# Two experts' weight tiles through one ring of seven buffers: the first nine loads of each pair in another order

## The reference

```python
for e in range(N_EXPERTS):
    out = out + gates[:, e:e + 1] * swiglu(tok, w_gate_up[e], w_down[e])
# swiglu(h, wgu, wd): gate, up = split(h @ wgu); (silu(gate) * up) @ wd
# wgu: 1024 x 7168, wd: 3584 x 1024, float32: 44 MB for each expert
```

## Time and profile before

| | |
|---|---|
| median of 3 executions | 1496.53 us (1495.41 to 1497.82) |
| the profiled execution, its own time | 1497.91 us |
| its span from the first to the last instruction | 1496.1 us |
| TensorE busy | 1346.0 us, 90% of the span |
| VectorE / ScalarE busy | 673.5 / 520.2 us |
| moved by DMA | 474.28 MB, mean 317 GB/s |

### The profile page before, as it was taken

How to read it: one execution, slowest core, us unless ns; L and a number is a source line. 1 busy time by engine, 2 the same in 40 slices (tenths; PEclk the granted TensorE clock), 3 DMA queues, 4 the chain that set the end, 5 groups by cost and what they waited for, 6 DMA issues and landing times.

```text
span 1496.1 us, 25369 instructions
## 1 busy us (share of the span) xinstructions
PE 1346.0 (90%) x11187; PEld 966.0 (65%) x11188; DVE 673.5 (45%) x754; ACT 520.2 (35%) x566; POOL 35.8 (2%) x66
## 2 busy tenths in 40 slices
PE   3899899999999897999999999999888889887776
PEld 2674578888789646777776777766675665443332
DVE  5953344445354526655453755443764553100002
ACT  2323433343253604444442454443553442000001
POOL 3000000000010002000000000000000000000000
PEclk8989999999999997999999999999998999999999
DMA  8874794554495214689999989999999999999994
GB/s 285 323 289 156 285 394 170 203 189 169 169 340 205 75 57 171 224 337 410 412 411 412 384 319 411 411 410 412 399 351 411 414 411 411 412 412 413 412 413 190
DMA packets 206791, 474.28 MB, mean 317 GB/s; under 512 B 9986, under 2 KB 10030, under 8 KB 206670
## 3 DMA queue, kind: packets, MB, share of 16 engines
q1 hardware_dynamic: 199968, 470.83, 81.2%
q10 hardware_dynamic: 6702, 1.71, 0.5%
HBM read 471.47 MB, written 1.05 MB: 316 GB/s over the span
## 4 chain that ended last, share of the span: by engine, by line
PE 64%; DMA 16%; SPq 12%; DVE 3%; ACT 2%; issue 1%; ACTq 1%; POOL 0%; POOLq 0%; DVEq 0%
PE ps L2355 39%; DMA ring<-in_moe_w_down_dram 13%; SPq L511 12%; PE ps L2667 6%; PE ps L2679 5%; DMA ring<-in_ada_w_dram 3%; PE ps L2528 2%; PE ps L2331 2%; PE ps L2166 1%; PE ps L2230 1%; PE ps L2291 1%; PE ps L2622 0%; PE ps L2659 0%; PE ps L2252 0%; PE ps L2456 0%
## 5 line engine op out<-in xcount | busy, mean ns | idle before, releaser
L1918 DVE TENSOR_TENSOR ring_lo<-ring,w 128x2048 fp32r<-128x2048 f32 x126 | 288.2, 2290 | 186.3 <-ACT w L1063 149.0
L1063 ACT ACTIVATE w<-ring 128x2048 fp32r<-128x2048 f32 x126 | 240.4, 1912 | 221.0 <-PE ps L2355 208.8
L2667 PE MATMUL ps<-ring,arena 128*32 128x128 f32 (+1 forms) x5376 | 240.2, 294 | 28.6 <-DMA ring<-in_moe_w_gate_up_dram 24.8
L2667 PEld LDWEIGHTS ps<-ring,arena 128*32 128x32 f32 (+1 forms) x5376 | 183.3, 115 | 89.2 <-DMA ring<-in_moe_w_gate_up_dram 34.8
L2355 PE MATMUL ps<-ring_lo,x_hi 128*128 128x512 f32 x592 | 231.2, 391 | 0.0
L2355 PE MATMUL ps<-w,x_hi 128*128 128x512 f32 x336 | 135.3, 403 | 4.5 <-DVE ring_lo L1918 2.6
L1541 DVE TENSOR_TENSOR ring_lo<-ring,w_hi 128x2048 fp32r<-128x2048 f32 x42 | 95.6, 2290 | 89.0 <-ACT w_hi L788 89.0
L2355 PE MATMUL ps<-w,x_lo 128*128 128x512 f32 x336 | 131.3, 391 | 0.0
L2355 PEld LDWEIGHTS ps<-ring_lo,x_hi 128*128 128x128 f32 x592 | 111.3, 188 | 21.2
L2679 PE MATMUL ps<-ring,tri 128*32 128x512 f32 (+1 forms) x448 | 72.6, 662 | 38.1 <-DMA ring<-in_moe_w_down_dram 36.1
L788 ACT ACTIVATE w_hi<-ring 128x2048 fp32r<-128x2048 f32 x42 | 78.8, 1908 | 49.1 <-PE ps L2355 42.1
(11 more groups left out here) (399 smaller groups left out, 1694.3 us busy)
## 6 DMA issues: line engine op xcount, KB each, us to landing
ring<-in_moe_w_gate_up_dram SPq DMA_DIRECT2D x112, 2048.0 KB, 17.5
ring<-in_moe_w_down_dram SPq DMA_DIRECT2D x56, 2048.0 KB, 18.3
ring<-in_ada_w_dram SPq DMA_DIRECT2D x24, 2048.0 KB, 11.1
ring<-in_ffn_w_gate_up_dram SPq DMA_DIRECT2D x14, 2048.0 KB, 11.6
ring<-in_ffn_w_down_dram SPq DMA_DIRECT2D x7, 2048.0 KB, 7.7
ring<-in_sb_w_qkv_dram SPq DMA_DIRECT2D x6, 2048.0 KB, 8.6
ring<-in_s_w_out_dram SPq DMA_DIRECT2D x2, 2048.0 KB, 7.7
ring<-in_sb_w_out_dram SPq DMA_DIRECT2D x2, 2048.0 KB, 14.5
```

Of the source, the lines that this page charges most:

```text
L1063: act.activation(half3(h).bitcast(F32R), ff_half(gran(pair_place(*main_granule(n))), half), ACT.Copy).then_inc(whi_done, 1)
L1918: dve.tensor_tensor(ff_half(ring_lo[place % RING][:, :], half).bitcast(F32R), ff_half(gran(place), half), half3(h), ALU.subtract).then_inc ...
L2667: ins = pe.matmul(dst[width * r:width * r + width, 0:cols], x[:, k, 0:width], weights[:, k, cols * r:cols * r + cols], start=k == 0, stop= ...
```

## The change

Positions 2 to 7 of each pair's list change places. Written out:

| position | 0 | 1 | 2 | 3 | 4 | 5 | 6 | 7 | 8 | 9 | 10 | 11 | 12 | 13 | 14 |
|---|---|---|---|---|---|---|---|---|---|---|---|---|---|---|---|
| buffer | 2 | 3 | 4 | 5 | 6 | 0 | 1 | 2 | 3 | 4 | 5 | 6 | 0 | 1 | 2 |
| before | ag0 | au0 | ag1 | au1 | ad0 | bg0 | ad1 | bu0 | ag2 | au2 | bg1 | ad2 | bu1 | ag3 | bd0 |
| after | ag0 | au0 | ad0 | ag1 | au1 | bg0 | bu0 | ad1 | ag2 | au2 | bg1 | ad2 | bu1 | ag3 | bd0 |

From position 8 on the lists are the same. The code that runs when the routing does not allow pairs took its places from position in the old list too; `expert_place` keeps the first five granules of that code in the buffers where the loads ahead now put them. That code isn't executed for these inputs.

```
 def pair_order():
 
-    order = [("ag", 0), ("au", 0), ("ag", 1), ("au", 1), ("ad", 0), ("bg", 0), ("ad", 1), ("bu", 0), ("ag", 2)]
+    order = [("ag", 0), ("au", 0), ("ad", 0), ("ag", 1), ("au", 1), ("bg", 0), ("bu", 0), ("ad", 1), ("ag", 2)]
     for f in range(2, FB):
         order += [("au", f), ("bg", f - 1), ("ad", f), ("bu", f - 1)]
         if f < FB - 1:
...
+def expert_place(g):
+
+    return N_MOE + {2: 3, 3: 4, 4: 2}.get(g, g)
...
-                swiglu_weights(moe_w_gate_up[0][0], moe_w_down[0][0], lambda g: N_MOE + g,
+                swiglu_weights(moe_w_gate_up[0][0], moe_w_down[0][0], lambda g: expert_place(g),
                                lambda g: (N_MOE + g) // RING, AHEAD)
...
-                                wait_used(act, N_MOE + gate_at(f), moe_turn(gate_at(f)))
+                                wait_used(act, expert_place(gate_at(f)), moe_turn(gate_at(f)))
```

More of the change, by code:

```diff
@@ L592, in _ @@
                     swiglu_weights(gate_up[bass.ds(expert * D, D), :], downs[bass.ds(expert * FF, FF), :],
-                                   lambda g: N_MOE + g, lambda g: e * (PER_EXPERT // RING) + (N_MOE + g) // RING)
+                                   lambda g: expert_place(g), lambda g: e * (PER_EXPERT // RING) + (N_MOE + g) // RING)
             for tt in range(TT):
@@ L1210, in w_round @@
                                 return
-                            wait_landed(act, N_MOE + g, moe_turn(g))
+                            wait_landed(act, expert_place(g), moe_turn(g))
                             if h >= 3:
@@ L1214, in w_round @@
                                 if part:
-                                    wait_used(act, N_MOE + before, moe_turn(before))
+                                    wait_used(act, expert_place(before), moe_turn(before))
                                 else:
                                     act.wait_ge(h0_read, split * PER_EXPERT + before + 1)
-                            act.activation(half3(h).bitcast(F32R), ff_half(gran(N_MOE + g), half), ACT.Copy
+                            act.activation(half3(h).bitcast(F32R), ff_half(gran(expert_place(g)), half), ACT.Copy
                                            ).then_inc(whi_done, 2 if g in plain else 1)
                         def silu_main(f):
-                            wait_used(act, N_MOE + gate_at(f), moe_turn(gate_at(f)))
+                            wait_used(act, expert_place(gate_at(f)), moe_turn(gate_at(f)))
                             if f:
@@ L2037, in product_item @@
                                 dve.wait_ge(m_silu, e * FB + f + 1)
-                                wait_used(dve, N_MOE + up_at(f), moe_turn(up_at(f)))
+                                wait_used(dve, expert_place(up_at(f)), moe_turn(up_at(f)))
                                 if f:
@@ L2065, in w_rest @@
                                 dve.wait_ge(*tail_read[g])
-                            dve.tensor_tensor(ff_half(ring_lo[(N_MOE + g) % RING][:, :], half).bitcast(F32R),
-                                              ff_half(gran(N_MOE + g), half), half3(h), ALU.subtract
+                            dve.tensor_tensor(ff_half(ring_lo[expert_place(g) % RING][:, :], half).bitcast(F32R),
+                                              ff_half(gran(expert_place(g)), half), half3(h), ALU.subtract
                                               ).then_inc(wlo_done, 2 if g in plain else 1)
@@ L2950, in gate_product @@
                         def gate_product(f, ch, width):
-                            n = N_MOE + gate_at(f)
+                            n = expert_place(gate_at(f))
                             wait_landed(pe, n, moe_turn(gate_at(f)))
@@ L2956, in up_product @@
                         def up_product(f, ch, width):
-                            n = N_MOE + up_at(f)
+                            n = expert_place(up_at(f))
                             wait_landed(pe, n, moe_turn(up_at(f)))
@@ L2982, in down_product @@
                         def down_product(f, ch, width):
-                            n = N_MOE + down_at(f)
+                            n = expert_place(down_at(f))
                             wait_landed(pe, n, moe_turn(down_at(f)))
@@ L3019, in tail_in @@
                         def tail_in(g, f, at, done):
-                            n = N_MOE + g
+                            n = expert_place(g)
                             wait_landed(pe, n, moe_turn(g))
@@ L3051, in halves @@
                         def halves(g, half, cols):
-                            low = ff_half(ring_lo[(N_MOE + g) % RING][:, :], half)
+                            low = ff_half(ring_lo[expert_place(g) % RING][:, :], half)
                             return [w.rearrange("p (k n) -> p k n", n=cols) for w in (half3(2 * g + half), low)]
                         def main_in(g, f, bank, free):
-                            n = N_MOE + g
+                            n = expert_place(g)
                             if f:
```

## The result

The changed kernel takes 1486.41 us (median of 4 executions, 1482.16 to 1487.72) against 1497.17 us for the kernel before (1495.41 to 1498.13): 10.8 us less, a ratio of 0.9925 with a 95% interval of 0.9902 to 0.9947. Measured a second time (6 executions beside 11 of the kernel before) the ratio was 0.9928 (0.9913 to 0.9942). Forecast were 9.5 us and 1487.0 us.

What follows compares the result with a forecast made beforehand. The routed SwiGLU was taken as bound by its 352 MB of weight loads, the winnable time being queue gaps. Terms of 2.5 + 2.7 + 4.3 = 9.5 us off 1496.5 gave 1487.0 us, range 1483.6 to 1492.2.

Steps and rivals of the forecast that it cites:

- The reading of the holes: Queue gaps at the start of pairs 0 to 2, of 20.2, 10.8 and 6.7 us: loads wait for buffers.
- The split into TensorE's half and the queue's: In a wide pair with a tail, PE sets the pace of the first half and DMA of the second.
- the lead: How much earlier loads land: 5.1 to 6.5 us in pair 0, cut to 1.7 to 3.2 after bu 2.
- Pair 0: Pair 0's share of the gain: 2.5 us (1.7 to 3.2), left after bu 2 and passed on to pair 1.
- Pair 1: Pair 1's share of the gain: 2.7 us (1.9 to 3.4), left after bu 2; PE's 4.4 us of waits cover it.
- Pair 2: Pair 2's share of the gain: 4.3 us, with ad 2 landing 3.7 to 4.5 us earlier.
- TensorE at pair 2's start: PE's down 0 product in pair 2: DVE's gate-up product precedes its splits, 0.2 us to gain, counted as nothing.
- The price of a starved load: A load issued into an empty queue lands 7.5 to 9.0 us later, mean 8.2.
- A: Rival: starved loads bg 2 and bu 2 cost 10.7 us or more, only pair 2 gains 4.3: 1492.2; chance 0.07.
- C: Rival: in pair 2 too the hole only moves, to bg 2 and bu 2; no measurable change, 1496 us; chance 0.07.
- B: Rival: starved loads at the lower price and PE's waits in pairs 0 to 2 used up: 12.9 us, 1483.6; chance 0.05.
- D: Rival: ad 1 late for ACT's split in each wide pair, 15.3 us lost if hit fully, 1502; chance 0.05.

Runs made afterwards that it cites:

- swap_only: Kernel before with only bu 0 and down 1 changing places in each pair's list: ratio 1.0008 to the kernel before.
- release_f2: Changed kernel with block 2 of the list also in order of release (bg1 au2 bu1 ad2), in all pairs: ratio 0.9927 to the kernel before.
- release_f23: Changed kernel with blocks 2 and 3 also in order of release: ratio 0.9900 to the kernel before, repeated 0.9893.
- pair2_only: Changed kernel with the new order in pair 2 alone, the old one in the other pairs: ratio 0.9969 to the kernel before.
- pairs01_only: Changed kernel with the new order in pairs 0 and 1 alone, the old one in the others: ratio 0.9969 to the kernel before.
- release_all: Changed kernel with blocks 2 to 6 of the list also in order of release: ratio 0.9931 to the kernel before.
- ad1_after_ag2: Changed kernel with down 1 one place later still, behind ag 2: ratio 0.9954 to the kernel before.

## Why the prediction was right

**The reading of the holes.** Right in each point: au 2 goes with ad 0's release, bg 1 with ag 1's, TensorE's releases before bd 2 stand unmoved to the hundredth (bu 2's issue), and swap_only shows that the other exchange in the nine places doesn't matter.

**The split into TensorE's half and the queue's.** This was the step that decided the size: 37.7 us of holes, a gain of 10.7. That the lead is capped at TensorE's unmoved releases was right, and release_f2 and release_f23 show it from the other side, as the gain grows when bu 2 and bu 3 no longer wait. That bu 2 is the tightest was not quite right in pair 0. The lead (landing in the kernel before less landing after, both from the landing of ag 2) is 2.9 us at bu 2, and 1.7 to 2.0 us from bd 1 to bu 3, whose releases don't move either. It is 3.0 at the next load, ag 5, because ag 5 landed 6.4 us behind bu 3 in the kernel before and 5.2 us in the one after.

**The terms.** Pair 0: forecast 2.5 us, in the trace 2.8. Pair 1: 2.7 and 3.1; at bu 2 it was 2.0, the rest came between the end of pair 1 and ag 2 of pair 2. Pair 2: 4.3 and 4.8. There I had let ad 2 wait for au 1's release; TensorE was further ahead of the queue than in the trace of before, and the hole closed completely. All three terms were a little low, the sum by 1.2 us. That the first two came out this near is partly luck, since single landings of the full queue, 5.1 us apart as a rule, come about 1.3 us late now and then: six are 6.1 to 6.4 us behind the last in the stream of the kernel before, five 6.0 to 6.6 in the one after. Why they do is not shown, and a term can't be confirmed more closely than one of them.

**TensorE at pair 2's start.** The prediction counted nothing there, as down 0's splits stood 0.2 us behind DVE's product in the trace of before. That holds only for a TensorE as late as in that trace. In pair2_only it began its product on down 0 5.1 us earlier than in the kernel before, counted from pair 0's ag 2; it was 4.8 us earlier already at its product on ag 0, for a reason not followed further, and in swap_only, 2.9 us earlier there, it still had to wait 4.7 us for down 0's split. Once pairs 0 and 1 had brought it forward, the old order would have held it at down 0 for 6.4 us (pairs01_only), and the new one held it for 1.9, by VectorE's order. The three terms were added as if they were independent, and this one coupling is worth the 1.2 us that did not add up.

**The price of a starved load.** 7.7, 8.0, 7.8 and 9.3 us after the change, inside the 7.5 to 9.0 that I had taken but for the last. The fit in the Trainium skill (SBUF — State Buffer, "The DMA setup-cost knee") gives an estimate of 6.8 us for this size, and none of the four is below 7.7: the measurement decides.

**The rivals.** A (only pair 2 pays) is out by pairs01_only, C (no change) by the time. B's 12.9 us were not reached by this change, but its bound wasn't the end of what an order of loads can win: release_f23 has 14.4 us by the stream, since with the lead kept TensorE no longer waits for DMA in pairs 0 and 1. Pair 0 alone won 5.3 us there, 1.2 more than its 4.1 us of waits; what makes up the difference is not shown. D's margin for down 1 was there: in the trace after, ScalarE began its split at 1074.47, 4.5 us after it had landed. DVE's order at the start of pair 2 held PE's down product as forecast: two splits, 4.49 us together, and a_lo straight behind the product of gate and up.

```profile
1055.43 0.69 DVE L1929 TENSOR_TENSOR arena<-arena,ps 128x512 f32<-128x512 f32 x1 [1.02 <-PE ps L2360]
1056.04 4.49 DVE L1923 TENSOR_TENSOR ring_lo<-ring,w 128x2048 fp32r<-128x2048 f32 x2
1060.44 0.68 DVE L1961 TENSOR_TENSOR a_lo<-ps,a_hi 128x512 fp32r<-128x512 f32 x1
```

## What to carry to other kernels

When a ring of buffers is filled by one queue in order, list the loads so that the buffers they wait for come free in that order, as long as the reader sets the pace. Where the queue sets it, list them in the order of first use: in this kernel release_all, with the order of release in the later blocks too, paid 5.6 us. A hole in the queue is worth only what is left of it where the pace changes hands: find the next load whose landing is least above the starved price, and the reader's waits behind it, and take the smaller. Gains in consecutive stages needn't add up: a reader that comes earlier can meet a wait that it didn't have. When single times spread by more than the effect, measure the affected stream inside the traces.

## What the runs showed of the hardware

TensorE's granted clock fell to its lower level of 1.2 GHz (0.5 of full speed) for 3.4 us behind short waits in an otherwise busy stretch. In the kernel before it did so behind PE's wait of 2.1 us for bd 3 of pair 1. The windows of that place:

```profile
990.00:995.00 5.00, 2.92 (x75) 1.99 (x77) 3.90 (x4) 2.56 (x3) 0.00 (x0) 1.00 1.03 405
995.00:1000.00 5.00, 5.00 (x22) 2.89 (x15) 0.01 (x1) 0.00 (x0) 0.00 (x0) 0.66 1.05 406
```

The same happened behind waits for DMA of 2.0 us in swap_only, 2.5 us in pair2_only, and 2.1 and 3.0 us in ad1_after_ag2, and behind PE's wait of 1.9 us for DVE at pair 2's start in the kernel after. Behind the wait of 1.4 us for bd 3 of pair 1 in the kernel after it did not fall, and neither did it behind waits of 2.6 us in pair 0 and of 2.3 us in pair 1 of the kernel before. So the length of a wait doesn't settle it. 3.4 us at half speed are 1.7 us of work: a microsecond saved on a wait can save that too, and not every time.

In the first 200 us, the same code was granted 0.91 or 0.92 of full speed in the trace of the kernel before and 0.94 to 0.96 in that of the one after, as shown with the result. The instruction of DVE that starts at 185.6 us in the kernel before starts between 177.2 and 185.6 us in the twelve traces, a spread as wide as that of the ninth load of pair 0 (615.4 to 623.3 us). So most of what makes single executions differ by several us lies in their first 185 us. That the clock is the reason in every one of them is not shown.
